# Five of the eight contraction tiles of an output projection are multiplied in plain fp32 inside the attention stage

## The reference, cut to what matters

```python
def fox_block(q, Fq, qpos, k, v, Ft, kpos):
    s = jnp.einsum("bqhd,bshd->bhqs", q, k) * (DH_C ** -0.5)
    s = s + jnp.swapaxes(Fq, 1, 2)[..., None] - Ft[:, :, None, :]
    s = jnp.where(qpos[:, None] >= kpos[None, :], s, -jnp.inf)
    p = jax.nn.softmax(s, axis=-1)
    return jnp.einsum("bhqs,bshd->bqhd", p, v)
...
# in trunk_layer
ha, C1, n1, m1 = mlstm(...)
hb, hist1 = pool_mix(...)
hc = fox_prompt(...)          # or fox_sample, with a paged cache of 2048 past positions a sequence
mix = jnp.concatenate([ha, hb, hc.reshape(B, T, W_C)], axis=-1).astype(x.dtype) @ w_out[l]
x = (x + g1 * mix).astype(x.dtype)
h2 = (rmsnorm(x, g_norm2[l]) * (1.0 + sc2) + sh2).astype(x.dtype)
ff = jnp.square(jax.nn.relu(h2 @ w_up[l])) @ w_down[l]
x = (x + g2 * ff).astype(x.dtype)
```

## Time and profile before

| | |
|---|---|
| median of three runs | 2899.29 us |
| the profiled execution, first to last instruction | 2905.2 us |
| TensorE busy | 2763.6 us (95%) |
| VectorE busy | 1186.2 us (41%) |
| ScalarE busy | 659.8 us (23%) |
| GpSimd busy | 424.7 us (15%) |
| mean granted clock of TensorE | 0.978 of 2.4 GHz |

### The profile page before, as it was taken

The page is one execution under the profiler, slowest core; times in us unless marked ns, Lnnn a source line. Parts: engine busy times, 40 slices in busy tenths (PEclk is TensorE's granted clock), DMA queues, the critical chain, the costliest instruction groups (busy, mean ns, idle before and its releaser), DMA issues. The chain is left out here.

```text
span 2905.2 us, 48336 instructions
## 1 busy us (share of the span) xinstructions
PE 2763.6 (95%) x20492; PEld 2553.9 (88%) x20492; DVE 1186.2 (41%) x2069; ACT 659.8 (23%) x1122; POOL 424.7 (15%) x424
## 2 busy tenths in 40 slices
PE   5999988889999999999999999878999999999998
PEld 3999965569999999999989999545899999999998
DVE  5625524346532422424355344333564233242344
ACT  4334323333111111001133432333231001001011
POOL 1101114340000000001111000244300001001010
PEclk9999989899999999999999999899999999999999
DMA  7440157741222222111224101776302111111111
GB/s 299 146 105 30 64 193 272 252 148 44 66 88 84 81 84 73 59 44 44 66 106 117 48 30 66 267 262 223 125 31 86 54 49 44 44 59 44 44 58 68
DMA packets 106873, 295.36 MB, mean 102 GB/s; under 512 B 19606, under 2 KB 32791, under 8 KB 104611
## 3 DMA queue, kind: packets, MB, share of 16 engines
q1 hardware_dynamic: 106498, 291.49, 29.8%
q0 software_dynamic: 160, 0.79, 0.1%
HBM read 269.61 MB, written 22.63 MB: 101 GB/s over the span
## 5 line engine op out<-in xcount | busy, mean ns | idle before, releaser
L304 PE MATMUL PS<-hH,whi 128*128 128x352 f32 x1632 | 533.2, 327 | 8.0 <-DVE hL L2193 6.4
L304 PE MATMUL PS<-hL,whi 128*128 128x352 f32 x1632 | 523.8, 321 | 0.0
L304 PE MATMUL PS<-hH,wlo 128*128 128x352 f32 x1632 | 523.4, 321 | 0.0
L304 PE MATMUL PS<-aH,whi 128*128 128x352 f32 x1344 | 439.6, 327 | 9.2 <-DVE aL L251 9.1
L304 PE MATMUL PS<-aL,whi 128*128 128x352 f32 x1344 | 432.7, 322 | 0.0
L304 PE MATMUL PS<-aH,wlo 128*128 128x352 f32 x1344 | 432.4, 322 | 0.0
L292 POOL CAST whi<-raw 128x1024 fp32r<-128x1024 f32 x158 | 167.6, 1061 | 1672.6 <-PE PS L304 1336.5
L304 PEld LDWEIGHTS PS<-hH,whi 128*128 128x128 f32 x1632 | 306.7, 188 | 16.7 <-issue 11.8
L304 PEld LDWEIGHTS PS<-hL,whi 128*128 128x128 f32 x1632 | 307.4, 188 | 0.0
L304 PEld LDWEIGHTS PS<-hH,wlo 128*128 128x128 f32 x1632 | 306.4, 188 | 0.0
L824 PE MATMUL PS<-aH,whi 128*128 128x352 f32 x912 | 303.7, 333 | 1.9 <-ACT F L1022 1.9
(11 more groups left out here) (353 smaller groups left out, 3840.8 us busy)
## 6 DMA issues: line engine op xcount, KB each, us to landing
KVp<-kv SPq DMA_DIRECT2D x256, 384.0 KB, 4.3
raw<-w_ff SPq DMA_DIRECT2D x128, 512.0 KB, 3.5
raw<-w_in SPq DMA_DIRECT2D x42, 512.0 KB, 3.5
wad_single<-w_ada SPq DMA_DIRECT2D x40, 512.0 KB, 3.5
wad<-w_ada SPq DMA_DIRECT2D x32, 512.0 KB, 5.5
x_spill<-x SPq DMA_DIRECT2D x2, 4224.0 KB, 13.9
wada<-w_first SPq DMA_DIRECT2D x8, 1024.0 KB, 7.2
raw<-w_out SPq DMA_DIRECT2D x16, 512.0 KB, 4.3
```

The source lines that it names most:

```text
L304: last = nc.tensor.matmul(PS[:, 3 * p + part, 0:CW], w[:, k, :], a[:, k, part * CW:(part + 1) * CW], start=k == 0 and w is wh and a is hig ...
```

## The change

Tiles 0 to 4 of the concatenation (READY = 5: the three rows of group A and the two of group B) are taken out of the output projection. Their product with `w_out` is done in the attention stage, in plain fp32 without halves: 24 pieces (8 output panels by 3 parts of 352 tokens), each of five accumulating matmuls. In even steps TensorE does piece i behind `query_key(i)` and piece i + 1 behind `turn(i - 1)`. ScalarE empties a piece; two panels stay in SBUF, six are stored to a buffer in memory, by DMAs that ScalarE issues. The weights of a panel (5 of 8 tiles) come through three buffers, loaded by SP between the pages. To make room the page ring shrinks from 24 to 20 buffers.

In the output projection the split, the weights and the contraction cover the three last tiles only. x and the stored partial sums come back in four pairs of rows. A new step of GpSimd, `join_part`, adds a panel's partial sum to what ScalarE emptied, and VectorE's `residual_part` waits for it.

The multiplication of the exponentials by 1/sum on GpSimd is gone: TensorE transposes the exponentials as they are, VectorE writes the reciprocals as a 128x128 tile, TensorE transposes it behind the unit's values, ScalarE copies that to SBUF (`inverse_out`) and VectorE multiplies the result of `mixed` by it.

```diff
-    kv0 = [small0 + 3072 * i for i in early + tuple(i for i in range(22) if i not in early)] + [aH0 + 3072 * i for i in range(2)]
+    kv0 = [small0 + 3072 * i for i in early + tuple(i for i in range(2, 22) if i not in early)]
...
+    READY = 5
+    DIRECT = {0: KC, 1: KC + 1}
+    PANELS = (2, 3, 4, 0, 5, 6, 1, 7)
...
                 for i in range(NB * STEPS):
                     b, step = divmod(i, STEPS)
+                    if i in (2, 4, 9, 13, 17, 21, 25):
+                        part_weights((2, 4, 9, 13, 17, 21, 25).index(i) + 1)
...
                 for i in range(NU):
-                    for e in range(2):
-                        n = (units[i][1] + 1) * P
-                        pool.wait_ge(S["shares"], i + 1)
-                        nc.gpsimd.tensor_scalar(Trow[i % 2][e][:, 0:n], Trow[i % 2][e][:, 0:n], sums[:, i % 4, e:e + 1], None, ALU.mult)\
-                            .then_inc(S["scaled"], 1)
...
+                def part_product(c):
+                    p, part = divmod(c, NCH)
+                    pe.wait_ge(part_loaded, 16 * (p + 1))
+                    for k in range(READY):
+                        last = nc.tensor.matmul(PS[:, 1 + 2 * (c % 2), 0:CW], wpart[p % 3][:, k, :], F[:, MIX[k], part * CW:(part + 1) * CW],
+                                                start=k == 0, stop=k == READY - 1)
+                    last.then_inc(S["part_done"], 1)
...
                         query_key(i)
+                        if i % 2 == 0:
+                            part_product(i)
                     b, part = divmod(i, 3)
                     if b < NB and part == 2:
                         past_mixed(b)
                     if 1 <= i <= NU:
                         turn(i - 1)
+                    if i < NU and i % 2 == 0:
+                        part_product(i + 1)
...
# mixed(u) of TensorE, VectorE and ScalarE
+                    pe.wait_ge(S["inverted"], u + 1)
+                    nc.tensor.transpose(PS[:, bank[key], P:2 * P], inverse[u % 2][:].rearrange("p e d -> p (e d)"), ident)
...
+                    dve.wait_ge(S["inverse_out"], u + 1)
+                    nc.vector.tensor_tensor(F[:, QC + j, qb * P:(qb + 1) * P], PS[:, bank[key], 0:P], norms[u % 2][:], ALU.mult).then_inc(S["dve"], 1)
...
-                        nc.vector.reciprocal(sums[:, i % 4, :], sums[:, i % 4, :]).then_inc(S["shares"], 1)
+                        wide = sums[:, i % 4, :].rearrange("p (e o) -> p e o", o=1).to_broadcast([P, 2, DH])
+                        nc.vector.reciprocal(inverse[i % 2][:], wide).then_inc(S["inverted"], 1)
...
# out_and_mlp
-                load_x(0)
+                def load_pair(i):
+                    if i >= 2:
+                        sp.wait_ge(pair_loaded[i % 2], landed_pair(i - 2))
+                    sp.dma_start(x[:, 2 * i:2 * i + 2, :], x_spill[:, 2 * i:2 * i + 2, :]).then_inc(pair_loaded[i % 2], 16)
+                    if i:
+                        for j in (2 * i, 2 * i + 1):
+                            sp.dma_start(mix_part[j][:], mix_parts[:, j, :]).then_inc(pair_loaded[i % 2], 16)
+                load_pair(0)
                 for n in range(2, AHEAD):
                     load(sp, n)
+                    if n < KT // 2 + 1:
+                        load_pair(n - 1)
...
+                def join_part(ph, j):
+                    pool.wait_ge(s["room"], (2 * (j + 1), 2 * KT + j + 1)[ph])
+                    if j >= 2 and ph == 0:
+                        pool.wait_ge(pair_loaded[j // 2 % 2], landed_pair(j // 2))
+                    t = ev[j % 2][:, COLS[ph]]
+                    nc.gpsimd.tensor_tensor(t, t, mix_part[j][:, COLS[ph]], ALU.add).then_inc(joined, 1)
+
                 for part in range(1, NCH):
-                    for k in range(KT):
+                    for k in range(READY, KT):
                         mix_high(part, k)
                     split_high(pool, part + 1)
-                for n in range(4, KT):
-                    split_high(pool, n)
+                for j in range(KT):
+                    join_part(0, j)
+                    if j < 4:
+                        split_high(pool, 4 + j)
+                for j in range(KT):
+                    join_part(1, j)
+                    if j < 2:
+                        split_high(pool, KT + j)
```

More of the change, by code:

```diff
@@ L296, in split_low, with part_product @@
             dve.wait_ge(s["high"], n + 1)
-            nc.vector.tensor_tensor(wl[:], raw[spot(n)][:], wh[:].bitcast(F32), ALU.subtract).then_inc(s["split"], 1)
+            nc.vector.tensor_tensor(wl[:, tiles(n)], raw[spot(n)][:, tiles(n)], wh[:, tiles(n)].bitcast(F32), ALU.subtract).then_inc(s["split"], 1)
         return s, load, split_high, split_low
-    def part_product(p, part, k, high, low, home=None):
+    def part_product(p, part, k, high, low, home=None, first=0):
         wh, wl = home or (whi[p], wlo[p])
@@ L304, in part_product @@
             last = nc.tensor.matmul(PS[:, 3 * p + part, 0:CW], w[:, k, :], a[:, k, part * CW:(part + 1) * CW],
-                                    start=k == 0 and w is wh and a is high, stop=k == KT - 1 and w is wl)
+                                    start=k == first and w is wh and a is high, stop=k == KT - 1 and w is wl)
         return last
@@ L1408, in trunk @@
     RING = len(kv0) // GP
+    READY = 5
+    wpart = [tile(f"wpart{i}", [P, READY, P], a) for i, a in enumerate((aH0, aH0 + 2560, small0 + 3072))]
+    part_row = [tile(f"part_row{i}", [P, CW], small0 + 4 * CW * i) for i in range(2)]
+    DIRECT = {0: KC, 1: KC + 1}
+    mix_rows = [16, 17, 8, 9, 10, 11, 12, 18]
+    mix_part = [tile(f"mix_part{j}", [P, TOK], row_at(r)) for j, r in enumerate(mix_rows)]
+    PANELS = (2, 3, 4, 0, 5, 6, 1, 7)
+    NPART = KT * NCH
     D0 = aH0 + 2 * 3072
@@ L1430, in trunk @@
     future = tile("future", [P, P], T0 + 256, BF16)
+    inverse = [tile(f"inverse{i}", [P, 2, DH], T0 + 512 + 512 * i) for i in range(2)]
+    norms = [tile(f"norms{i}", [P, P], T0 + 1536 + 512 * i) for i in range(2)]
     units = [(j, qb) for j in range(PAIRS) for qb in (0, 7, 2, 5, 1, 6, 3, 4)]
@@ L1465, in slot_table @@
             if i >= 2:
-                take(("mixed", i - 2), "act")
+                take(("mixed", i - 2), "dve")
             if i == 0:
@@ L1484, in attention @@
     def attention(l):
-        names = ("filled", "act", "dve", "qk", "low", "exp", "shares", "scaled", "chain", "zero", "query", "cumulated", "fill", "min", "past_exp", "pad",
-                 "past_mixed", "gap", "share", "weights", "selected", "masks")
+        names = ("filled", "act", "dve", "qk", "low", "exp", "inverted", "inverse_out", "chain", "zero", "query", "cumulated", "fill", "min", "past_exp", "pad",
+                 "past_mixed", "gap", "share", "weights", "selected", "part_done", "part_out")
         S = {n: sem(f"fox_{n}") for n in names}
@@ L1492, in attention @@
         kvl = [sem(f"fox_kv{i}") for i in range(RING)]
+        part_loaded = sem("fox_part_loaded")
+        part_stored = [sem(f"fox_part_stored{i}") for i in range(2)]
         hp = lambda e: slice(64 * e, 64 * e + 64)
@@ L1504, in has_room @@
                 is_empty(pe, slots[index[key] - 4][0])
+        stored_before = lambda c: sum(PANELS[m // NCH] not in DIRECT for m in range(c % 2, min(c, NPART), 2))
         with nc.Block() as block:
@@ L1591, in query_key @@
                     if i == 0:
-                        pe.wait_ge(S["masks"], 2)
+                        pe.wait_ge(S["zero"], 2)
                     for e in range(2):
@@ L1901, in _ @@
                     if i >= 2:
-                        mixed(i - 2)
+                        inverse_out(i - 2)
+                    if i < NU and i % 2 == 0:
+                        part_store(i + 1)
                     if b < NB and part == 0:
@@ L1907, in _ @@
                         nc.scalar.activation(share[:], share[:], ACT.Exp).then_inc(S["share"], 1)
+                for i in range(2):
+                    act.wait_ge(part_stored[i], 16 * stored_before(NPART + i))
     def out_and_mlp(l):
@@ L2022, in third @@
                 def third(n, part, operands, tile_ready=None, half=None):
-                    for k in range(KT):
+                    first_k = READY if n < KT else 0
+                    for k in range(first_k, KT):
                         if tile_ready:
                             tile_ready(k)
-                        last = part_product(n % 2, part, k, *operands, home(n))
+                        last = part_product(n % 2, part, k, *operands, home(n), first_k)
                         if half and k == 4:
@@ L2248, in by_phases @@
                             if ph == 0:
-                                if run == 0 and j < KT // 2:
-                                    mix_low(2, 2 * j)
-                                    mix_low(2, 2 * j + 1)
+                                if run == 0 and j < LATE:
+                                    mix_low(2, READY + j)
                                 if j + 2 < KT:
```

(6 more changed lines are left out.)

108 lines of the change are left out of this document (73 added, 35 removed).

## The result

The changed kernel takes **3046.94 us** (3046.39 to 3050.07, 4 runs) against 2900.44 us (2896.34 to 2910.07), a ratio of 1.050, 95% interval [1.0482, 1.0519]. The prediction was 2973 us, range 2900 to 3025: the side was right, the size half of what came.

What follows compares the result with a forecast made beforehand. TensorE, busy 95% of 2905.2 us, was the bound. Attention 71.0 + 2.9 - 14.7 - 3.0 + 5 - 9 = +52 us a layer, projection -15, two layers +74: 2979, less 5.9: 2973 us, range 2900 to 3025.

Steps and rivals of the forecast that it cites:

- (c): Rival: page ring and ring of joins both at their upper ends, attention +75, projection -10, 3029 us; chance 0.15.
- part 3: Attention, page ring: first wait covered, -3.0 us; later pages +5 us a layer, between -10 and +21.
- The bound of +75: Attention: upper bound of the forecast growth of +52 us a layer; the lower bound was +25.
- part 2: Attention, late division: GpSimd waits gone, -14.7 us; transposes +2.9; VectorE's reciprocal taken as 0, 12 kept for the range.
- Part 1: Attention, moved products in plain fp32: 24 pieces x 5 x 2 x 0.296 = +71.0 us a layer at full clock.
- part 4: Attention, TensorE's clock: pieces fill gaps, the ring makes new ones; -9 us a layer, from 0 to -22.
- Rival (b): Balance: page ring costs nothing more (attention +37), ring of joins doesn't bind (-31 to -37); 2903 us, chance 0.10.
- Part 5, phase 0: Output projection: GpSimd's queue closes a ring of joins, 7.5 us a turn; phase 0 ends at about 51 us.
- The chain: Output projection, between phases 0 and 1: 11 us before, gets a join, 13 us forecast.
- Phase 1: Output projection: 22.5 us stay because VectorE has 19.9 us of work; 2.5 of waits taken off in the sum.

Runs made afterwards that it cites:

- stub_ring20: Changed kernel, 20 page buffers, one weight tile for all pieces, partial sums not stored (right weights and sums left out): 3033.03 us, 1.0467.
- stub_ring24: Changed kernel, one weight tile for all pieces, partial sums not stored (right weights and sums left out), 24 page buffers again: 2962.30 us, 1.0211.
- ring20_alone: Kernel before with 20 page buffers instead of 24 and nothing else: 2973.76 us, 1.0255.
- after_piece_behind: Changed kernel with the mixing ahead of the piece where a step has both, four steps a layer: 3003.63 us, 1.0345.
- after_split_first: Changed kernel; VectorE splits the next weight panel before the residual, second MLP panel cast at join 4 of phase 1, not join 1: 3020.19 us, 1.0415.

## Why the prediction was wrong, by its own steps

**The account.** 3046.9 - 2900.4 = 146.5 us are 70.7 for the ring (stub with 20 less stub with 24), 13.9 for the pieces' loads and stores (of two sessions, so a few us unsure), and 61.9 for the rest: pieces, late division and projection. By layer the attention grew by 33 us (stub with 24), 34 for the ring and 10 for the transfers: 78 with rounding, where the prediction has +52. The projection and all else gave back 5 to 7 us, where it has 15. Two layers of both, (26 + 9) x 2 = 70, are nearly the whole miss. Of the rivals (c), with +75 and -10 (3029 us, chance 0.15), came nearest, and the result lies beyond it.

**The step that failed is part 3, the page ring**, as the prediction put it: "Against this the stretch gets one piece after even batches and two after odd ones", and from it +5 us in place of the +21 of its own upper end. It had the term itself right: twelve pages in place of eight, 1.08 us each, 4.3 us more a batch, seven times a layer: 30.2 us. The runs show this term in full. From the start of a mixing to the end of the next scores it is 16.1 us on average in the kernel before, 20.3 in ring20_alone, 20.4 in stub_ring20, 20.8 in the changed kernel and 20.7 in after_piece_behind: with 20 buffers the pages set this stretch, whatever TensorE does in it. With the slower clock beside it the ring costs 33 and 36 us a layer in the stubs, 29 and 37 alone. What failed is the cover. The prediction took the idle time before the scores as the whole price of late pages, and let the pieces hide most of it. But release, transfer, scores, softmax and mixing are a round, and the round is what takes time. A piece between mixing and scores hides; a piece between scores and mixing adds to the round itself, and 12 of the 24 stand there. after_piece_behind moves four a layer and nothing else, and returns 22 to 26 us a layer.

Read off the profiles of before and after, the 26 us that the attention is over its forecast are some 12 us of waits for pages (they rose by 14 us a layer, where -3.0 + 5 stood in the sum) and 16 us of busy time (it rose by 81, where 71.0 + 2.9 - 9 stood), less 2 elsewhere. With +21 and no gain of clock the same sum gives +77. The bound of +75 was below this sum of its own upper ends, and 12 us that part 2 kept for the range weren't in it.

**Part 1** (+71.0): the pace was right (ten records in 3.12 us at full clock, 2.96 from start to start). The busy time in layer 1 is 83.3 us in the changed kernel (x240, 499 ns mean) and 79.9 with 24 buffers, as a part of the records runs at the lower clock (a piece then takes up to 4.9 us where the rows above show 3.1); part 1 had full clock throughout and left the rest to part 4.

**Part 2** (-14.7 + 2.9): the wait for GpSimd went, and nothing was gained. Alone it came to -4 us in one layer and +3 in the other. "I take away all that TensorE waits for it" was the error. The question "what is late next" had its answer in the same rows, pages and ScalarE's copies.

**Part 4** (-9 for the clock): 0.89 and 0.90 granted, as before; with 24 buffers 0.95. The gain was there to have and needs the waits gone. The Trainium skill (TensorE: Matmul & The Clock Gate, "HAM oscillation") has the array cold again after waits between bursts; the traces agree, 0.90 with 27.5 us of page waits and 0.95 with 0.5 us.

**Parts 1 to 4 without the ring** came to +33 us a layer in stub_ring24, where my terms without the ring's 5 make +47. Rival (b), with +37, is nearest to that kernel, which also lacks the loads and stores. So the sum held two errors of opposite sign, and that it missed by no more is luck: with a full ring the pieces fill more than I gave them, and with the small one they don't cover it.

**Part 5, phase 0**, was right in its mechanism and 4 us short: 55.4 us (51), the first five joins 7.2 us apart on average, each behind a cast that waited for its load. TensorE was busy for 37.6 us of it, over half where under half was forecast, at a granted clock of 0.72. In GpSimd's order of time:

```profile
2215.30 0.50 POOL L293 CAST ohi<-raw 128x384 fp32r<-128x384 f32 x1 [5.34 <-DMA raw<-w_out]
2215.77 1.68 POOL L2077 TENSOR_TENSOR ev<-ev,mix_part 128x704 f32<-128x704 f32 x1
2222.35 0.50 POOL L293 CAST ohi<-raw 128x384 fp32r<-128x384 f32 x1 [4.90 <-DMA raw<-w_out]
2222.81 1.68 POOL L2077 TENSOR_TENSOR ev<-ev,mix_part 128x704 f32<-128x704 f32 x1
```

The join took 1.68 us; 2.0 was taken, and the estimate from the Trainium skill (GPSIMD Engine Reference, section 3.1) was 1.55, the closer of the two. The chain took 12.5 us (13). **Phase 1** was missed: 25.4 us where 20 was in the sum (22.5 less 2.5). It has a second ring. The MLP's second panel is loaded into the buffer that the first one holds until VectorE splits it, its cast stands in GpSimd's queue ahead of join 2, and join 2 is waited for by the residual that stands ahead of TensorE's next free banks:

```profile
2267.68 1.04 POOL L293 CAST whi<-raw 128x1024 fp32r<-128x1024 f32 x1 [5.58 <-DMA raw<-w_ff]
```

The rule that found the ring in phase 0 (list what stands ahead in each in-order queue, and follow it round) was not carried on into phase 1. after_split_first opens both: in its trace the time up to phase 1's first join is 11 to 13 us shorter a layer, and from there to the last join 2 to 4 us, of which 13 us a layer reach the total.

**What stays open.** after_piece_behind returned 43 us where pieces times places give 24 to 32. Of the 48 us that its two attentions are shorter in the traces, 26 are waits for pages and 25 busy time at the same number of matmuls, so the clock (0.94 and 0.93 for 0.89 and 0.90), with 3 us more of other waits; why a moved piece gives back more than its own length is argued from this, not tested. Whether a second queue that issues pages would shorten the twelve pages' 12.9 us wasn't tried. Whether keys released earlier would help wasn't tried in a form that leaves the rate alone. The changed kernel in its better orders with 24 buffers and real weights doesn't fit as laid out; by the stub (2962) and the 27 us of split_first it would be at some 2935 us, an estimate, still above the kernel before.

## What to carry to other kernels

Price a smaller prefetch ring as a round: (pages more to fetch between release and use) x (queue time of one) x (turns, without the first, which needs no release), and add what the longer waits cost in clock. Count as cover only work that stands between the release and the use; independent work ahead of the releasing instruction lengthens the round, so put the release first and the filler behind it, but never behind it what starts the next dependent chain. Before filling a gap, ask what the filler's buffers are taken from: 12 KB a partition, taken for weights and rows, cost 71 us here, and 3 KB more for pages was the only edit that won.

## What the runs showed of the hardware that was not expected

The cost of a page load in the queue did not go by its bytes: 1.08 us for 384 KB in rows of 3 KB (128 partitions) and 1.11 us for 192 KB in rows of 1.5 KB, back to back, so that halving the transfers cut the rate in the attention from 237 to 172 GB/s. Both have 128 rows, so no run tells a price for each DMA from one for each row, or says whether whole pages were held at 1.08 us by something else. A GpSimd add of 352 columns took 0.93 us in the chain, where VectorE was busy 7.7 of 12.5 us, and 1.53 in the last four joins of phase 1, a phase in which it was busy 20.6 of 25.4; adds of 704 columns took 1.68 us, and 2.1 to 2.3 in some of the later joins. That VectorE's work slows them is argued, not tested.
